# Thirteen of sixteen experts in descending order of their token counts, with 128 down to 80 slots

## The reference, cut to what matters

```python
gates = jnp.sum(jax.nn.one_hot(expert_id, N_EXPERTS, dtype=F32)
                * (p_g[:, None] * top_w)[..., None], axis=1)
h = jax.nn.silu(jnp.einsum('nd,edf->nef', xf, w_g)) * jnp.einsum('nd,edf->nef', xf, w_u)
out = jnp.einsum('nef,efd->nd', h * gates[..., None], w_d)
```

## Time and profile before

| | |
|---|---|
| median of 3 runs | 569.36 us (568.02 to 569.65) |
| the profiled execution | 567.37 us, its span 565.3 us |
| busy: PE, PEld, DVE, ACT, POOL | 97%, 63%, 38%, 29%, 17% of the span |
| chain that ended last, by engine | PE 90%, DVE 5%, DMA 2%, rest 3% |
| the expert loop on PE | from 358.6 to 544.8 us, 16 experts |
| mean granted TensorE clock | 0.995; 1.00 in every stretch of the loop |
| transfers | mean 236 GB/s over the span, 324 to 352 in most of the loop |

### The profile page before, as it was taken

One profiled execution on the slowest core, in us unless ns is written; L12 is line 12 of the kernel. 1 busy time (PEld: TensorE's weight loads), 2 busy tenths in 40 slices (PEclk: granted clock), 3 DMA queues, 4 the chain that ended last, 5 costly groups with the idle time before them and its releaser, 6 DMA issues.

```text
span 565.3 us, 7700 instructions
## 1 busy us (share of the span) xinstructions
PE 548.0 (97%) x3042; PEld 355.4 (63%) x3042; DVE 215.0 (38%) x544; ACT 162.1 (29%) x310; POOL 98.1 (17%) x116
## 2 busy tenths in 40 slices
PE   8899999999999999999999998999999999999994
PEld 6577755544454455565444444878888788877851
DVE  3435386422222333326333755524223232222138
ACT  7332676712122132222223154111111111111132
POOL 3016000134000000003100202332322333232100
PEclk8999999999999999999999999999999999999999
DMA  9999997899400000069510239899999999999674
GB/s 282 356 334 336 330 363 318 299 387 334 168 1 0 0 1 1 0 231 352 164 56 37 83 115 361 239 304 350 350 330 328 340 352 350 341 324 346 191 205 169
DMA packets 73640, 133.21 MB, mean 236 GB/s; under 512 B 4154, under 2 KB 49634, under 8 KB 71554
## 3 DMA queue, kind: packets, MB, share of 16 engines
q1 hardware_dynamic: 59008, 99.36, 50.9%
q0 software_dynamic: 9536, 28.75, 18.3%
q10 hardware_dynamic: 5058, 4.58, 2.4%
HBM read 117.47 MB, written 18.35 MB: 240 GB/s over the span
## 4 chain that ended last, share of the span: by engine, by line
PE 90%; DVE 5%; DMA 2%; issue 1%; ACT 1%; SPq 1%; ACTq 0%
PE psum L723 86%; PE psum L726 4%; DMA ring<-in_w_mod_dram 2%; DVE arena L2192 1%; DVE x L2197 1%; SPq L509 0%; DVE arena L2111 0%; ACT uT L1360 0%; ACT arena L1360 0%; ACTq L1600 0%; DVE uT L1774 0%; DVE gst L1982 0%; DVE arena L2055 0%; DVE arena L2067 0%; DVE rtb L2111 0%
## 5 line engine op out<-in xcount | busy, mean ns | idle before, releaser
L723 PE MATMUL psum<-ring,uT 128*128 128x512 f32 (+1 forms) x384 | 126.5, 522 | 0.0
L723 PEld LDWEIGHTS psum<-arena,ring 128*128 128x128 f32 x1024 | 116.8, 192 | 8.4 <-issue 8.4
L723 PE MATMUL psum<-arena,ring 128*128 128x128 f32 x1024 | 117.0, 275 | 1.0 <-DVE arena L2250 1.0
L1360 ACT ACTIVATE arena<-psum 128x512 f32<-128x512 f32 (+6 forms) x95 | 44.9, 495 | 230.5 <-PE psum L723 160.7
L723 PEld LDWEIGHTS psum<-ring,uT 128*128 128x128 f32 (+1 forms) x384 | 56.5, 172 | 60.1 <-issue 55.8
L723 PE MATMUL psum<-uT,ring 128*128 128x288 f32 x256 | 64.9, 410 | 1.3 <-ACT uT L1360 1.3
L723 PE MATMUL psum<-ring,arena 128*128 128x512 f32 x128 | 58.7, 602 | 0.0
L723 PEld LDWEIGHTS psum<-uT,ring 128*128 128x128 f32 x256 | 47.7, 190 | 17.5 <-issue 5.1
L1360 ACT ACT_TABLE_LOAD x33 | 42.3, 1283 | 3.1 <-issue 2.1
L2296 DVE TENSOR_TENSOR arena<-arena,psum 128x128 f32<-128x128 f32 x32 | 9.2, 288 | 86.9 <-PE psum L723 86.9
L723 PEld LDWEIGHTS psum<-ring,arena 128*128 128x128 f32 x128 | 23.0, 190 | 23.0 <-issue 23.0
(11 more groups left out here) (216 smaller groups left out, 455.3 us busy)
## 6 DMA issues: line engine op xcount, KB each, us to landing
ring<-in_w_mod_dram SPq DMA_DIRECT2D x24, 1024.0 KB, 11.7
ring<-in_w_exp_gate_dram SPq DMA_DIRECT2D x16, 1024.0 KB, 15.2
ring<-in_w_exp_up_dram SPq DMA_DIRECT2D x16, 1024.0 KB, 15.5
ring<-in_w_exp_down_dram SPq DMA_DIRECT2D x16, 1024.0 KB, 13.0
ring<-in_w_in_dram SPq DMA_DIRECT2D x10, 1024.0 KB, 10.6
ring<-in_w_out_dram SPq DMA_DIRECT2D x4, 1024.0 KB, 7.1
f_dram<-in_consts_dram POOLq DMA_DIRECT2D x1, 3072.0 KB, 19.4
arena<-in_state_ret_dram POOLq DMA_DIRECT2D x6, 512.0 KB, 5.5
```

Source lines behind the costliest of these rows:

```text
L723: return nc.tensor.matmul(out, lhsT, rhs, start=first, stop=last)
L1360: return nc.scalar.activation(out, src, func, **kw).then_inc(done, 1)
```

## The change

Experts 0, 1 and 2 run first with 128 slots as before. The other thirteen run in descending order of their counts; the expert at position e has `SLOTS_AT[e]` slots: 128 at position 3, then 124, 120 and so on down to 80 at position 15 (312 fewer than 2048 in all). VectorE makes the order on the chip: `find_places` compares the 13 counts in pairs (13 x 13 = 169 elements a row), and puts the largest of count + 4 x position in `count1`, so that the other path is taken when a list doesn't fit its slots; `find_order` makes the permutation `perm` and the table `order` of expert numbers; `sort_columns` applies it to `rank1` and to `gates` (new tiles `rankp`, `gatep`). SyncE reads an expert number from `order` for each of the thirteen and loads the weights from the address that follows from it. Gathers, one-hot matrices, transposes, projections and results use n slots instead of 128. The gate weights, made before `take_input(0)` up to now, are made after it and after `new_state(2)` and `new_state(3)`.

```diff
+FIXED = 3
+SORTED = NE - FIXED
+FEWER = 4
+SLOTS_AT = [P - FEWER * max(0, e - FIXED) for e in range(NE)]
...
+            def load_chosen(e):
+
+                which = sp.value_load(order[0:1, e - FIXED:e - FIXED + 1], min_val=0, max_val=NE - 1)
+                for kind, w, n in (("wg", w_exp_gate, FE), ("wu", w_exp_up, FE), ("wd", w_exp_down, D)):
+                    p = (kind, e, 0)
+                    sp.wait_ge(*used[before[p]])
+                    sp.dma_start(ring[:, slot[p], :].rearrange("p (k n) -> p k n", n=n),
+                                 w[0, bass.ds(which, 1)].rearrange("a (k p) n -> p (a k) n", p=P))\
+                        .then_inc(landed[slot[p]], 16)
...
-                for p in late:
-                    load(p)
+                sp.wait_ge(s_order, 1)
+                for e in range(FIXED, NE):
+                    load_chosen(e)
...
                 for t in range(TILES):
-                    last = mm(bank[7][:, 128:129], hit[e % 2][:, t, :], tok[:, t:t + 1],
+                    last = mm(bank[7][0:n, 128:129], hit[e % 2][:, t, 0:n], tok[:, t:t + 1],
                               t == 0, t == TILES - 1)
...
-                        last = turn(bank[2 + k // 4][:, (k % 4) * P:(k % 4 + 1) * P],
-                                    xg[e % 2][:, k * P:(k + 1) * P])
+                        last = turn(bank[2 + k // 4][:, (k % 4) * P:(k % 4) * P + n],
+                                    xg[e % 2][0:n, k * P:(k + 1) * P])
...
-                                last = mm(out, w[:, k, m * P:(m + 1) * P], xgT[e % 2][:, k, :],
+                                last = mm(out, w[:, k, m * P:(m + 1) * P], xgT[e % 2][:, k, 0:n],
...
+                n = SLOTS_AT[e]
+                shape = [P, TILES, n]
+                at = rank1 if e < FIXED else rankp
+                v.tensor_tensor(out=hit[e % 2][:, :, 0:n],
+                                in0=con[:, None, C_IOTA:C_IOTA + n].to_broadcast(shape),
+                                in1=at[:, :, e:e + 1].to_broadcast(shape),
                                 op=ALU.is_equal).then_inc(s_hit, 1)
...
+            pairs = [P, SORTED, SORTED]
+
+            def find_places():
+
+                big = key[:, FIXED:]
+                tt(perm[:], big[:, None, :].to_broadcast(pairs), big.unsqueeze(2).to_broadcast(pairs),
+                   ALU.is_gt)
+                link(v.tensor_reduce(out=place[:, FIXED:], in_=perm[:], axis=AX.X, op=ALU.add))
+                link(v.scalar_tensor_tensor(out=key[:], in0=place[:], scalar=float(FEWER),
+                                            in1=tally[:], op0=ALU.mult, op1=ALU.add))
+                link(v.tensor_reduce(out=count1, in_=key[:], axis=AX.X, op=ALU.max))
+
+            def find_order():
+
+                tt(perm[:], place[:, None, FIXED:].to_broadcast(pairs),
+                   con[:, C_IOTA:C_IOTA + SORTED].unsqueeze(2).to_broadcast(pairs), ALU.subtract)
+                link(v.tensor_scalar(perm[:], perm[:], -1.0, None, ALU.is_equal))
+                tt(mixed[:, 0:SORTED, :], perm[:],
+                   con[:, None, C_IOTA + FIXED:C_IOTA + NE].to_broadcast(pairs), ALU.mult)
+                link(v.tensor_reduce(out=key[:, 0:SORTED], in_=mixed[:, 0:SORTED, :], axis=AX.X,
+                                     op=ALU.add))
+                v.tensor_scalar(order[:], key[:, 0:SORTED], -1.0, None, ALU.add).then_inc(s_order, 1)
...
+            def sort_columns(nth_sort, out, src):
+
+                link(v.tensor_copy(out[:, :, 0:FIXED], src[:, :, 0:FIXED]))
+                for t in range(TILES):
+                    rows_t = slice(t * SORTED, (t + 1) * SORTED)
+                    v.tensor_tensor(out=mixed[:, rows_t, :], in0=perm[:],
+                                    in1=src[:, t, None, FIXED:].to_broadcast(pairs),
+                                    op=ALU.mult).then_inc(s_sorted, 1)
+                dve.wait_ge(s_sorted, TILES * (nth_sort + 1))
+                return v.tensor_reduce(out=out[:, :, FIXED:],
+                                       in_=mixed.rearrange("p (t r) e -> p t r e", r=SORTED),
+                                       axis=AX.X, op=ALU.add)
+
+            dve.wait_ge(s_tl, 3 * MT + 3)
             hits(0)
+            link(v.scalar_tensor_tensor(out=key[:], in0=tally[:], scalar=float(NE),
+                                        in1=con[:, C_REV:C_REV + NE], op0=ALU.mult, op1=ALU.add))
+            find_places()
             v.tensor_scalar(over[:], count1, float(CAPACITY), None, ALU.is_gt).then_inc(s_over, 1)
             numbers(0)
...
-                for e in range(1, AHEAD):
-                    hits(e)
-                    numbers(e)
-
+                hits(1)
+                find_order()
+                numbers(1)
+                hits(2)
+                link(sort_columns(0, rankp, rank1))
+                numbers(2)
+                take_input(0)
+                for h in range(2, NH):
+                    new_state(h)
                 gate_weights()
                 dve.wait_ge(s_gw, 1)
                 w16 = lambda w: w.unsqueeze(2).to_broadcast([P, TILES, NE])
-                v.tensor_tensor(out=oh[0], in0=oh[0], in1=w16(rm1), op=ALU.mult).then_inc(s_fb, 1)
-                v.tensor_tensor(out=oh[1], in0=oh[1], in1=w16(rm2), op=ALU.mult).then_inc(s_fb, 1)
-                dve.wait_ge(s_fb, 2)
-                v.tensor_tensor(out=gates[:], in0=oh[0], in1=oh[1], op=ALU.add).then_inc(s_gw, 1)
-                take_input(0)
-                for h in range(2, NH):
-                    new_state(h)
+                tt(oh[0], oh[0], w16(rm1), ALU.mult)
+                tt(oh[1], oh[1], w16(rm2), ALU.mult)
+                tt(gates[:], oh[0], oh[1], ALU.add)
+                sort_columns(1, gatep, gates).then_inc(s_gw, 1)
                 for e in range(NE):
```

More of the change, by code:

```diff
@@ L206, in build @@
         over = sb("over", [P, 1], I32)
+        order = sb("order", [P, SORTED], I32)
+        key = sb("key", [P, NE])
+        tally = sb("tally", [P, NE])
+        place = sb("place", [P, NE])
+        perm = sb("perm", [P, SORTED, SORTED])
         slot_tok = sb("slot_tok", [P, NE], U32)
@@ L1243, in expert_in @@
                         pe.wait_ge(s_hm, FT * e)
-                    for w, outs in ((wg, (bank[0][:, 0:P], bank[0][:, P:FE])),
-                                    (wu, (bank[1][:, 0:P], bank[6][:, 0:P]))):
+                    for w, outs in ((wg, (bank[0][:, 0:n], bank[0][:, P:P + n])),
+                                    (wu, (bank[1][:, 0:n], bank[6][:, 0:n]))):
                         if e == 0 and w is wu:
@@ L1262, in expert_out @@
                         for c in range(2):
-                            last = mm(bank[4 + c][:], hT[e % 2][:, k * P:(k + 1) * P],
+                            last = mm(bank[4 + c][0:n], hT[e % 2][:, k * P:k * P + n],
                                       wd[:, k, c * 512:(c + 1) * 512], k == 0, k == FT - 1)
@@ L1291, in add_last @@
                         o = slice(512 * c, 512 * c + 512)
-                        row = eo[(NE - 1) % 2][:, o]
+                        n = SLOTS_AT[NE - 1]
+                        row = eo[(NE - 1) % 2][0:n, o]
                         if t == TILES - 1:
-                            last = mm(summed[t][c * NS:(c + 1) * NS, 0:HALF], pT[:, t, 0:NS], row,
+                            last = mm(summed[t][c * NS:(c + 1) * NS, 0:HALF], pT[0:n, t, 0:NS], row,
                                       True, True)
                         else:
-                            last = mm(summed[t][:, o], pT[:, t], row, True, t in ON_DVE)
+                            last = mm(summed[t][:, o], pT[0:n, t], row, True, t in ON_DVE)
                         if t not in ON_DVE:
@@ L2084, in _ @@
             v.memset(logit[:], 0.0).then_inc(s_tl, 1)
-            dve.wait_ge(s_tl, 3 * MT + 1)
+            v.memset(place[:], 0.0).then_inc(s_tl, 1)
+            dve.wait_ge(s_tl, 3 * MT + 2)
             dve.wait_ge(s_qkT, TILES)
@@ L2168, in numbers @@
                 dve.wait_ge(s_tokn, e + 1)
-                found = bank[7][:, 128:129]
-                v.tensor_scalar(slot_tok[:, e:e + 1], found, 1.0, -1.0, ALU.max, ALU.add)\
+                n = SLOTS_AT[e]
+                found = bank[7][0:n, 128:129]
+                v.tensor_scalar(slot_tok[0:n, e:e + 1], found, 1.0, -1.0, ALU.max, ALU.add)\
                     .then_inc(s_idx, 1)
-                link(v.tensor_scalar(spare, found, 0.0, con[:, C_SPARE:C_SPARE + 1],
+                link(v.tensor_scalar(spare[0:n], found, 0.0, con[0:n, C_SPARE:C_SPARE + 1],
@@ L2307, in _ @@
                             v.tensor_scalar(wlast[:, t], con[:, C_IOTA:C_IOTA + P],
-                                            rank1[:, t, NE - 1:NE], gates[:, t, NE - 1:NE],
+                                            rankp[:, t, NE - 1:NE], gatep[:, t, NE - 1:NE],
                                             ALU.is_equal, ALU.mult).then_inc(s_last, 1)
```

67 lines of the change are left out of this document (40 added, 27 removed).

## The result

| | before | after |
|---|---|---|
| median of the runs | 568.73 us | 601.35 us |
| the profiled execution, its span | 567.37, 565.3 us | 607.94, 605.9 us |

The ratio is 1.048, 95% interval 1.044 to 1.052. The forecast was 572.8, its range 569.0 to 575.6. The ratio rests on the three executions of 594.6 to 597.3 us; the median in the table contains two longer ones of 605.4 and 607.9 us, and the second of these is the profiled one, so its stalls are some us more than a usual execution has.

The account below looks back on a forecast made before the run. The prediction took TensorE, with 90% of the chain of waits, as the bound; +1.8 (first expert) + 0.6 (gates) - 2.1 (transposes) + 3.1 (slot numbers) = +3.4 us on the median of 569.36 gave 572.8, range 569.0 to 575.6.

Parts of the forecast that it names:

- "Fewer gathered and added rows help", weights at 0: Weight loads and indirect transfers: register loads before each expert's transfers cost 0, and fewer gathered and added rows help.
- The prediction's own sign of being wrong: In the expert loop: TensorE waiting for a transfer of weights would show the forecast wrong.
- the room that weights have: SyncE's weight loads: the last is issued at 520.16 to 523.4 us for use near 541.8, so register loads fit.
- Projections at 0: Projection matmuls, positions 4 to 15: weight loads stay at 128 columns, so fewer moving columns save 0; bound -17.0 us.
- Transposes, -2.1: TensorE's transposes, narrower by 312 columns in all over twelve positions: -2.1 us, bounds 0 and -3.9.
- Slot numbers, +3.1: Slot-number matmuls: loads under 128 columns take the ordinary slope, 90 ns apart instead of 26: +3.1 us.
- The half-way cost named in the second rival: Slot-number matmuls: narrow loads cost half the ordinary slope, 22 ns each, 1.1 us; within the fast-load rival, 17%.
- The flag, +1.2: VectorE's chain before the flag gets longer; the flag starts at 351.68 instead of 350.46: +1.2 us, bounds 1.0 to 1.5.
- The first expert, +1.8: Start of the first expert, behind VectorE's ordering and sorting: 360.4 instead of 358.62, +1.8 us, flag included.
- The gates, +0.6: Gate weights made later: their gather lands at 377.9 to 380.6, a stall of 0 to 1.9 us, taken as 0.6.
- that the clock falls: Clock rival, TensorE in the loop: a fall to 1.2 GHz would add up to 11.7 us an expert; 2%.

Follow-up runs that it names:

- all_rows: The changed kernel with all 128 rows in every gather of inputs and gates, every addition to the output and the slot numbers: 569.3 us, ratio 1.002.
- sixteens: The changed kernel with every slot count rounded up to a multiple of 16 (128, 112, 96, 80), nothing else: 570.5 us, ratio 1.004.
- before_120: The kernel before the change, with 120 instead of 128 rows in all gathers of inputs and gates and all additions: 580.2 us, ratio 1.021.
- narrow_adds: The changed kernel with 128 rows in gathers and slot numbers, its own counts (124, 120, 116, ...) in the additions alone: 580.2 us, ratio 1.022.
- before_124_add: The kernel before the change, with 124 rows in the additions to the output only, both gathers keeping 128: 668.1 us, ratio 1.177.
- fixed_loads: The changed kernel with the late experts' weights loaded at fixed addresses in number order, without register loads: 599.1 us, ratio 1.053.

## Why the prediction was wrong, step by step

- **"Fewer gathered and added rows help", weights at 0: wrong, and the whole error.** Fewer rows did not help unless their number had the divisor 16: 112 rows gave 0.2% (0.0 to 0.4). 124 rows put 31 on each of four engines. The proof is all_rows: with this step undone the time is 569.3. The prediction's own sign of being wrong, TensorE waiting for a transfer of weights, is what came.
- **Its second half, the room that weights have: wrong too.** The earlier trace rows showed when the last load is issued; I should have read the DMA share of 1.06 beside it, and the 3.84 us (median, up to 10.12) that SyncE takes to issue a transfer of `wu`, as a queue without slack. The share by itself is not the loss (all_rows has 1.07 from 400 to 500 us and loses nothing there); it says that nothing is left for dearer transfers. Even all_rows waits 0.78 us once for a late piece, and sixteens 0.27 to 0.69 us six times.
- **Projections at 0: right.** 64 take 7.30 us with 124 columns and 7.27 with 80, against 7.31. The load of the weights sets the pace.
- **Transposes, -2.1: right.** Eight with 88 rows take 0.61 us, from 531.02 to 531.63, against 0.87.
- **Slot numbers, +3.1: the mechanism right, the size wrong.** The groups with 116 and with 80 columns, then the mean of one matmul in each:

```profile
406.13 0.38 PE L750 MATMUL psum<-tok,arena 128*116 128x1 f16 x5
...
531.63 0.32 PE L750 MATMUL psum<-tok,arena 128*80 128x1 f16 x5
...
L750 PE MATMUL psum<-tok,arena 128*116 128x1 f16 x5 | 0.4, 187 | 0.0
L750 PE MATMUL psum<-tok,arena 128*80 128x1 f16 x5 | 0.3, 175 | 0.0
```

  (0.38 - 0.187)/4 is 48 ns apart with 116 columns, (0.32 - 0.175)/4 is 36 with 80, against 26 with 128. Every narrow load is slower than the one of 128 columns, as the Trainium skill has it (page "TensorE: Matmul & The Clock Gate", section "Weight-path perf modes — Fast Weight Load (FWL) and DoubleRow": the fast load is on for 128 weights of a type other than FP32). But they cost about half of what I took from float32 loads, 102 ns with 116 columns and 72 with 80, and less than the 85 ns that the prediction worked out from the Trainium skill for 102. On average 16 ns are added (22 with 116 columns, 10 with 80): 12 x 4 x 16 = +0.8 us. The half-way cost named in the second rival, 22 ns, was nearest.
- **The flag, +1.2: right.** Counted from `sel`, it comes 4.10 us later (350.03 to 354.13) instead of 2.92: +1.18.
- **The first expert, +1.8: right.** 12.80 us after `sel` (362.83) instead of 11.08 (347.54 to 358.62): +1.72.
- **The gates, +0.6: 0.** In all_rows the down projections start at 370.24, 381.91 and 393.57, 11.67 and 11.66 apart, as before. VectorE took the gates at 378.09, within the forecast landing; the second expert's down projection, which waits for the copy that starts there, begins at 381.91, 3.8 us later.
- **Sum without the transfers:** +1.7 + 0 - 2.1 for all_rows, which moves full slot numbers; with its stall of 0.8 that is +0.4, measured +1.2 (0.1 to 2.2). Rivals: none of mine named the transfers, and that the clock falls had 2% but as its own cause; it came as an effect of the stalls.

**Open:** why 120 rows cost 2% though no engine has more to do. In before_120 the share of the DMA engines from 400 to 500 us is 1.07 with 302 GB/s, against 1.06 with 339 before, and the landings of a weight transfer are spread evenly over 6.7 us, without a late group. The page of the Trainium skill cited above says that k consecutive engines are taken "from a round-robin cursor", so the idle one would change from transfer to transfer; no run here shows that. Open are also why gathers make the weights late enough to stall TensorE and additions hardly, and how the 12 us of narrow_adds divide over its counts.

## What to carry to other kernels

Before you change the number of rows of a transfer, find the number of DMA engines that it will go over, the largest divisor up to 16, and the rows on each: cut in sixteens, or leave the transfer whole and narrow only the arithmetic. "Nothing waits for a transfer" says nothing about slack; read the share of the DMA engines and the landing times beside it, and ask what a transfer that takes longer holds up in its own queue. And when one engine is made faster, check whether a second one, here the DMA engines at 1.06, is full as well.

## What the runs showed of the hardware

- From 375 to 550 us an addition of 124 rows of 4096 B landed after 18.1 us (before_124_add, median of 10) instead of 9.1; additions of 122 rows followed each other after 28.5 us. Fewer bytes took twice as long.
- A few loaded engines delay a transfer that uses all sixteen: with 124 rows in the indirect transfers twelve pieces of a weight transfer landed within 2.2 us and the other four after 6.4 to 7.1.
- GpSimd itself needs longer to issue an uneven one: 1.60 us for an addition of 128 rows, 2.24 for 124, 2.97 for 122.
- A stall can cost more than its own time: at the stalls of 6.20, 3.81 and 6.67 us the clock went to 0.5, and 2.8, 1.7 and 9.6 us were lost on top; at those of 1.31 to 2.89 us it did not fall. The length of the stall alone doesn't decide it: in fixed_loads 64 matmuls took 13.93 us behind one of 2.81.
